# Decoder step: one weight transfer order, new-token values and sigmoid placement changed

## The reference

```python
mod = (silu(c) @ w_ada + b_ada)               # six shift/scale/gain vectors
h = x * (1 + sc1) + sh1
qa, ka, va, qb, kb, vb, ga, gb = split(h @ w_in)
# branch A: three groups of dilated attention, merged by their softmax denominators; branch B: block attention
# for a sample row the keys and values are [cached rows, the 4 new rows of its own sequence]
oa, ob = mixer(q, k, v)                        # 4 heads x 64 each
merged = sigmoid(ga) * (oa @ w_pa) + sigmoid(gb) * (ob @ w_pb)
x = layer_norm(ALPHA * x + g1 * (merged @ w_o))
f = (silu(gt) * up) @ w_down                   # up, gt = split(h2 @ w_up)
y = layer_norm(ALPHA * x + g2 * f)
```

## Time and profile before

| | |
|---|---|
| median of 3 runs | 548.4 us (546.83 to 549.36) |
| the profiled execution | 547.36 us, its span 545.8 us, TensorE's mean granted clock 0.981 |
| TensorE matmul busy | 505.8 us, 93% |
| VectorE, ScalarE, GpSimd busy | 290.1 (53%), 223.0 (41%), 89.0 us (16%) |
| chain that ended last | TensorE 76%, DMA 10%, VectorE 4%, SP's queue 3% |
| moved by DMA | 116.75 MB, 214 GB/s over the span |

### The profile page before, as it was taken

The page is one execution under the profiler, slowest core; times in us unless marked ns, Lnnn a source line. Parts: engine busy times, 40 slices in busy tenths (PEclk is TensorE's granted clock), DMA queues, the critical chain, the costliest instruction groups (busy, mean ns, idle before and its releaser), DMA issues.

```text
span 545.8 us, 9902 instructions
## 1 busy us (share of the span) xinstructions
PE 505.8 (93%) x3859; PEld 460.2 (84%) x3859; DVE 290.1 (53%) x548; ACT 223.0 (41%) x370; POOL 89.0 (16%) x127
## 2 busy tenths in 40 slices
PE   3989999998999799998999799999999999999980
PEld 1578988888788698895999599999999999999980
DVE  0266675757435354343875767545544544346356
ACT  1145333315434544356434455464444443333311
POOL 1000111126900000000244408210011100000005
PEclk9999999999999899999999889999999999999996
DMA  8999995495768920655443717997678754354002
GB/s 272 406 409 373 392 323 203 161 375 161 260 217 253 344 81 1 202 189 177 133 143 98 248 54 236 366 317 249 230 253 262 266 190 162 115 180 169 1 0 86
DMA packets 81356, 116.75 MB, mean 214 GB/s; under 512 B 3595, under 2 KB 59083, under 8 KB 80804
## 3 DMA queue, kind: packets, MB, share of 16 engines
q1 hardware_dynamic: 79428, 102.76, 55.4%
q0 software_dynamic: 1888, 13.44, 6.9%
HBM read 112.90 MB, written 13.57 MB: 232 GB/s over the span
## 4 chain that ended last, share of the span: by engine, by line
PE 76%; DMA 10%; DVE 4%; SPq 3%; issue 2%; ACT 2%; POOL 1%; POOLq 0%; ACTq 0%; DVEq 0%
PE psum L721 21%; PE psum L723 19%; PE psum L722 19%; DMA raw<-in_w_in 6%; DMA raw<-in_w_up 4%; PE psum L742 3%; PE psum L871 3%; PE psum L987 2%; PE psum L973 1%; DMA ada_s<-in_w_ada 1%; PE psum L756 1%; ACT w_hi L484 1%; PE psum L931 1%; PE psum L940 1%; PE psum L885 1%
## 5 line engine op out<-in xcount | busy, mean ns | idle before, releaser
L489 DVE TENSOR_TENSOR w_lo<-raw,w_hi 128x1024 fp32r<-128x1024 f32 (+1 forms) x120 | 147.0, 1227 | 157.2 <-ACT w_hi L484 156.8
L721 PE MATMUL psum<-act_hi,w_hi 128*128 128x288 f32 x736 | 223.2, 303 | 7.1 <-DVE act_lo L1753 2.9
L722 PE MATMUL psum<-act_lo,w_hi 128*128 128x288 f32 x736 | 218.4, 297 | 0.0
L723 PE MATMUL psum<-act_hi,w_lo 128*128 128x288 f32 x736 | 217.8, 296 | 0.0
L484 ACT ACTIVATE w_hi<-raw 128x1024 fp32r<-128x1024 f32 (+1 forms) x120 | 124.6, 1041 | 121.9 <-PE psum L723 93.2
L721 PEld LDWEIGHTS psum<-act_hi,w_hi 128*128 128x128 f32 x736 | 139.4, 189 | 20.2 <-issue 14.3
L723 PEld LDWEIGHTS psum<-act_hi,w_lo 128*128 128x128 f32 x736 | 139.8, 190 | 0.0
L722 PEld LDWEIGHTS psum<-act_lo,w_hi 128*128 128x128 f32 x736 | 139.7, 190 | 0.1
L721 PE MATMUL psum<-f_hi,w_hi 128*128 128x288 f32 x176 | 52.4, 298 | 0.6 <-DVE f_t L1790 0.6
L722 PE MATMUL psum<-f_lo,w_hi 128*128 128x288 f32 x176 | 51.9, 295 | 0.0
L723 PE MATMUL psum<-f_hi,w_lo 128*128 128x288 f32 x176 | 51.8, 294 | 0.0
(11 more groups left out here) (194 smaller groups left out, 560.7 us busy)
## 6 DMA issues: line engine op xcount, KB each, us to landing
raw<-in_w_up SPq DMA_DIRECT2D x22, 1024.0 KB, 5.8
ada_s<-in_w_ada SPq DMA_DIRECT2D x20, 1024.0 KB, 10.4
raw<-in_w_in SPq DMA_DIRECT2D x17, 1024.0 KB, 7.8
raw<-in_w_down SPq DMA_DIRECT2D x10, 1024.0 KB, 5.1
out<-in_cache_kv_a POOLq DMA_DIRECT2D x16, 504.0 KB, 6.4
raw<-in_w_ada SPq DMA_DIRECT2D x4, 1024.0 KB, 6.7
raw<-in_w_o SPq DMA_DIRECT2D x4, 1024.0 KB, 4.9
raw<-in_w_in SPq DMA_DIRECT2D x4, 768.0 KB, 12.9
```

What stands on the lines that cost most here:

```text
L489: nc.vector.tensor_tensor(part(w_lo, slot4, by_rows), raw_half(rslot, hh, by_rows), part(w_hi, slot4, by_rows).bitcast(F32), ALU.subtract) ...
L721: nc.tensor.matmul(out, hi_l, hi_r, start=start, stop=False, skip_group_check=True)
L722: nc.tensor.matmul(out, hi_l, lo_r, start=False, stop=False, skip_group_check=True)
L723: return nc.tensor.matmul(out, lo_l, hi_r, start=False, stop=stop, skip_group_check=True)
```

## The change

Four things change. (1) In SP's queue `GATE0 + 2` goes ahead of the keys of sequence 5, `GATE0 + 3` and `GATE0 + 4` go ahead of the values of sequence 0, `GATE0 + 5` ahead of the values of sequence 2, and `GATE0 + 6` ahead of a wait for GpSimd's stores and the values of sequences 3 and 4. (2) The new tokens' sample values are multiplied once, in a step 11 (`sample_new`), and their rows are picked by a third 0/1 table. (3) VectorE adds the three picked parts, so TensorE gathers one part in 4 matmuls; `own_rows` runs in steps 9, 12 and 14, and in step 14 ahead of `out_copy`. (4) ScalarE makes the first sigmoids after step 15 and puts the three copies of outputs between sigmoids. The table of constants is 4 columns wider.

```diff
--- before.py
+++ after.py
@@ -116,7 +116,7 @@
 C_MB1 = C_MA0 + 384
 C_EPS = C_MB1 + 256
 C_SELM = C_EPS + 1
-C_SEL = C_SELM + 8
+C_SEL = C_SELM + 12
 C_W32 = C_SEL + SAMPLE
 C_END = C_W32 + 32
 
@@ -138,6 +138,7 @@
     c[:, C_W32:C_W32 + 32] = 1.0 / 32
     b, h, t = row_of(np.arange(128))
     c[:, C_SELM:C_SELM + 8] = (b // 4 * 4 + h)[:, None] == np.arange(8)[None, :]
+    c[:, C_SELM + 8:C_SELM + 12] = h[:, None] == np.arange(4)[None, :]
     c[:, C_SEL:C_SEL + SAMPLE] = (b * DEC_T + t)[:, None] == np.arange(SAMPLE)[None, :]
     return c
 
@@ -393,7 +394,7 @@
     tok_turned, v_tok, k_tok = sem("tok_turned"), sem("v_tok"), sem("k_tok")
     kt_turned, kt_x, kt_y, scored_s = sem("kt_turned"), sem("kt_x"), sem("kt_y"), sem("scored_s")
     max_s, exp_s, prob_s = sem("max_s"), sem("exp_s"), sem("prob_s")
-    probT_turned, probT_s, pv_s = sem("probT_turned"), sem("probT_s"), sem("pv_s")
+    probT_turned, probT_s, pv_s, own_added = sem("probT_turned"), sem("probT_s"), sem("pv_s"), sem("own_added")
     scored, maxed, exped, turned, prbT_a, prbT_b, pv_done, o_ready = (sem(n) for n in (
         "scored", "maxed", "exped", "turned", "prbT_a", "prbT_b", "pv_done", "o_ready"))
     oT_turned, oT_h, oT_l = sem("oT_turned"), sem("oT_h"), sem("oT_l")
@@ -664,22 +665,23 @@
         load_kv(3, 0)
         sp.wait_ge(tok_turned, 11)
         load_kv(4, 0)
+        load_static(GATE0 + 2)
         for b in range(5, DEC_B):
             sp.wait_ge(kt_turned, b)
             load_kv(b, 0)
-        load_static(GATE0 + 2)
+        load_static(GATE0 + 3)
+        load_static(GATE0 + 4)
         for b in range(2):
             sp.wait_ge(kt_turned, 14 + b)
             load_kv(b, 1)
-        load_static(GATE0 + 3)
+        load_static(GATE0 + 5)
         sp.wait_ge(scored_s, 4)
         load_kv(2, 1)
-        load_static(GATE0 + 4)
+        load_static(GATE0 + 6)
         sp.wait_ge(stored_k, 16 * N_POOL_STORES)
         load_kv(3, 1)
-        load_static(GATE0 + 5)
         load_kv(4, 1)
-        for n in range(GATE0 + 6, PAB0 + 1):
+        for n in range(GATE0 + 7, PAB0 + 1):
             load_static(n)
         sp.wait_ge(pv_s, 1)
         for b in range(5, DEC_B):
@@ -915,14 +917,18 @@
                 if n in (3, 7, 9):
                     mm.then_inc(probT_turned, 1)
 
+        def sample_new():
+            pe.wait_ge(masked_s, 1)
+            for g in range(4):
+                mm = nc.tensor.matmul(psum[:, 7, 256 * (g // 3):256 * (g // 3) + 256], s_prbT[0:SAMPLE, 6 + g, :],
+                                      tok[0:SAMPLE, 2, 1, 256 * g:256 * g + 256], start=(g == 0), stop=(g >= 2),
+                                      skip_group_check=True)
+            mm.then_inc(pv_s, 1)
+
         def sample_values(half):
 
             if half == 1:
-                pe.wait_ge(masked_s, 1)
-            for g in range(4):
-                nc.tensor.matmul(psum[:, 7, 256 * (g // 3):256 * (g // 3) + 256], s_prbT[0:SAMPLE, 6 + g, :],
-                                 tok[0:SAMPLE, 2, 1, 256 * g:256 * g + 256], start=(g == 0), stop=False,
-                                 skip_group_check=True)
+                pe.wait_ge(masked_s, 2)
             for q in range(4):
                 place, before = kv_place(4 * half + q, 1)
                 pe.wait_ge(kv_in[place], 16 * KV_LOADS * (before + 1))
@@ -930,7 +936,7 @@
                 for q in range(4):
                     mm = nc.tensor.matmul(psum[32 * q:32 * q + 32, 7, 256 * br:256 * br + 256],
                                           s_prbT[0:nr, n, 32 * q:32 * q + 32], kv_tiles(4 * half + q, 1, tile)[0:nr, 0, :],
-                                          start=False, stop=(n == 5), skip_group_check=True)
+                                          start=(n == 0), stop=(n in (3, 5)), skip_group_check=True)
             mm.then_inc(pv_s, 1)
 
         def score(u, i, n):
@@ -1014,17 +1020,17 @@
                 prompt_values(s - 4)
             if s in (8, 13):
                 sample_values(s // 13)
+            if s == 11:
+                sample_new()
             if s == 14:
                 pe.wait_ge(o_ready, 8)
                 pe.wait_ge(maxed, 16)
                 outputs_turn(0)
 
-        pe.wait_ge(masked_s, 2)
+        pe.wait_ge(own_added, 1)
         for f in range(4):
-            for half in range(2):
-                mm = nc.tensor.matmul(psum[:, 7, SAMPLE * f:SAMPLE * f + SAMPLE], o_masked[:, half, 128 * f:128 * f + 128],
-                                      cst[:, C_SEL:C_SEL + SAMPLE], start=(f == 0 and half == 0), stop=(half == 1),
-                                      skip_group_check=True)
+            mm = nc.tensor.matmul(psum[:, 7, SAMPLE * f:SAMPLE * f + SAMPLE], o_masked[:, 0, 128 * f:128 * f + 128],
+                                  cst[:, C_SEL:C_SEL + SAMPLE], start=(f == 0), stop=True, skip_group_check=True)
         mm.then_inc(sel_done, 1)
 
         ada_ring(pe, ADA1)
@@ -1318,15 +1324,9 @@
                 softmax_exp(s - 2)
             if 3 <= s < N_UNITS + 3:
                 prbT_copy(s - 3)
-            if s == 14:
-                act.wait_ge(acc_free[0], 18)
-                act.wait_ge(acc_free[1], 18)
-                sigmoids(22, 24)
-                sigmoids(28, 32)
-            if s == 15:
-                sigmoids(12, 14)
-                sigmoids(24, 28)
-                sigmoids(14, 18)
+        act.wait_ge(acc_free[0], 18)
+        act.wait_ge(acc_free[1], 18)
+        sigmoids(22, 24)
 
         def oT_leading(br):
             act.wait_ge(oT_turned, br + 1)
@@ -1338,8 +1338,12 @@
         act.wait_ge(sel_done, 1)
         nc.scalar.activation(oT_hi[:, :, PROMPT:TOK], psum[:, 7, 0:4 * SAMPLE].rearrange("p (k c) -> p k c", c=SAMPLE),
                              ACT.Copy).then_inc(oT_h, 1)
+        sigmoids(28, 32)
         oT_leading(1)
+        sigmoids(12, 14)
+        sigmoids(24, 28)
         ada_rows(10)
+        sigmoids(14, 18)
         for h in range(4):
             hi_static(act, H_PAB + h + AHEAD)
             if h % 2 == 1:
@@ -1643,16 +1647,25 @@
                                       small[:, 96 + r0 + i:97 + r0 + i], None, ALU.mult)
             ins.then_inc(o_ready, 1)
 
-        def own_rows(half):
-
-            dve.wait_ge(pv_s, half + 1)
-            if half == 0:
+        def own_rows(part):
+
+            dve.wait_ge(pv_s, part + 1)
+            if part == 0:
                 dve.wait_ge(scored, scored_by(7))
-            pick = cst[:, C_SELM + 4 * half:C_SELM + 4 * half + 4].unsqueeze(2).broadcast_to([128, 4, E])
+            c = C_SELM + (0, 8, 4)[part]
+            pick = cst[:, c:c + 4].unsqueeze(2).broadcast_to([128, 4, E])
+            dst = min(part, 1)
             for br in range(2):
-                ins = V.tensor_tensor(o_masked[:, half, 256 * br:256 * br + 256].rearrange("p (j e) -> p j e", e=E),
+                ins = V.tensor_tensor(o_masked[:, dst, 256 * br:256 * br + 256].rearrange("p (j e) -> p j e", e=E),
                                       psum[:, 7, 256 * br:256 * br + 256].rearrange("p (j e) -> p j e", e=E), pick, ALU.mult)
             ins.then_inc(masked_s, 1)
+            if part > 0:
+                dve.wait_ge(masked_s, part + 1)
+                ins = V.tensor_tensor(o_masked[:, 0, :], o_masked[:, 0, :], o_masked[:, 1, :], ALU.add)
+                if part == 2:
+                    ins.then_inc(own_added, 1)
+                else:
+                    link(ins)
 
         def oT_rest(br):
             dve.wait_ge(oT_h, 1 if br == 0 else 3)
@@ -1672,11 +1685,13 @@
                 softmax_max(s - 2)
             if 3 <= s < N_UNITS + 3:
                 prbT_copy(s - 3)
+            if s == 14:
+                own_rows(2)
             if s >= 4:
                 out_copy(s - 4)
             if s == 9:
                 own_rows(0)
-            if s == 14:
+            if s == 12:
                 own_rows(1)
         oT_rest(0)
         dve.wait_ge(oT_h, 2)
```

## The result

| | before | change |
|---|---|---|
| median | 547.99 us (546.83 to 549.36, 4 runs) | 541.01 us (539.16 to 543.92, 4 runs) |
| ratio, 95% interval | | 0.9876, 0.9842 to 0.991 |
| profiled execution | 547.36 us | 540.16 us, its span 538.6 us |
| mean granted clock | 0.981 | 0.980 |

The change is faster, by 7.0 us on the medians; the forecast was 540.6. Over all executions, those timed later too, the mean is 540.13 us for the change (16) and 547.90 for before (60), 7.8 us apart.

The account below looks back on a forecast made before the run. TensorE, busy 93% of the span, was taken to bound the kernel. Terms of -3.5, -1.4, -1.9, -0.95, -1.4, +0.95 and +0.4 sum to -7.8 us, giving 540.6 us on the median, range 537.5 to 544.5.

Parts of the forecast that it names:

- (a): TensorE's wait for the first probabilities: with gate weights issued earlier it goes entirely, -3.5 us.
- (b): Gate products behind the wait for the first probabilities: TensorE's half clock there goes, -1.4 us.
- second rival: First probabilities: ScalarE's and VectorE's order, not the weight transfer, makes the softmax late; 545.5 us, chance 6%.
- (c): Sample products of steps 8, 11 and 13: new tokens' values multiplied once, one of two groups goes, -1.9 us.
- (d): Gather of sample outputs on TensorE: one part gathered, 8 of 16 passes stay, -0.95 us.
- (e): Before the first products with w_pa: output copies between sigmoids end TensorE's wait, -1.4 us.
- first rival: Behind the first w_pa products: VectorE's and ScalarE's own order takes the last gain back; 542.0 us, chance 13%.
- (f): Before prompt_values(11): VectorE's picking ahead of out_copy(10) makes TensorE go later, +0.9 us (0.94).
- third rival: Behind the idle before prompt_values(11): a new stretch at half clock loses 2.0 us; 542.6 us, chance 8%.
- (g): Key turns: keys of sequences 5 to 7 queue behind a 1 MB block, +0.4 us, bounds nothing and 2.9.
- So the block fits, but hardly: DMA between 137 and 143: room for 1.28 MB takes GATE0 + 2 ahead of the keys of sequences 5 to 7.
- last rival: Key turns: three gate blocks share DMA, keys up to 8.7 us late with half clock; 553.1 us, chance 3%.

Follow-up runs that it names:

- queue order alone: The kernel before with only the change's new order of weight blocks in SP's queue; 544.42 us, ratio 0.9935.
- the part alone: The change with SyncE's and ScalarE's programs as before, so only the sample products and VectorE's part changed; 546.48 us, ratio 0.998.
- ScalarE's order alone: The kernel before with only ScalarE's sigmoids moved so that output copies go between them; 547.86 us, ratio 1.0.
- two ahead: The change with GATE0 + 3 also ahead of the keys of sequences 5 to 7; 548.38 us, ratio 1.0009.
- the keys first: The change with GATE0 + 2 back behind the keys of sequence 7, GATE0 + 3 and + 4 right behind it; 541.24 us, second time 539.48 us.
- the addition behind: The change with VectorE's last addition of picked parts put behind out_copy(10); 540.31 us, second time 540.09 us.

## Why the prediction was right, point by point

(a), (b) **Right.** -3.5 and -1.4 predicted, -3.6 and -1.5 in the trace, and queue order alone gives the same to 0.02 us. How near (a) came is in part luck: the wait it removes was 3.47, 3.37 and 2.29 us in the three profiles with before's order of the gate blocks. The softmax was not late by itself (second rival): with `GATE0 + 4` early the probabilities came in time in every kernel that had it. The half clock behind the wait went with the wait.

(c) **Right in size**, -1.9 predicted and -1.8 measured. The moved group costs 2.06 us in step 11, where it had cost 1.92; step 13 with 1.92 us less cover did not wait. In the times of the part alone it can't be told from nothing.

(d), (e) **Right.** -0.95 and -1.4 predicted, -2.4 together in the trace; ScalarE's order alone gives -1.5. The first rival (the gain taken back behind the first products) is refuted: the stage behind kept its length to 0.03 us with or without it.

(f) **Mechanism right, the term too large by a quarter of a us; a stretch at half clock follows in part of the executions.** The way to the gather grew by 0.69 us where 0.94 was predicted; the wait is the 1.1 us of the list. The addition took 0.69, as the row it was priced by. VectorE's row of work took 2.07 us (245.10 to 247.17) where 2.15 was reckoned, it began 0.14 us after TensorE's last turn where 0.23 was reckoned, and the gather followed the start of the values after 0.47 us where before had 0.57; these three make up the 0.25. The wait became 1.08 where about 1.2 was said. But in four of seven profiles a stretch at half clock followed, which took another 1.5 us. That is what the third rival describes, with a chance of 8% and a price of 2.0; it came more often than that and cost a little less, though that the wait alone brings it isn't shown. Where it came, the profiled executions (538.88 to 540.90 us) stayed inside the range.

(g) **The step that was mis-sized: "So the block fits, but hardly".** In the change's own profiles it cost 0.1, 0.0 and 0.3 us where 0.4 was forecast, which is right. In two of six profiles with that queue order it cost 6.1 and 5.7 us, and the upper bound, 2.9, was too low; a wait for keys of 2 us or more was the prediction's own sign of being wrong. The bound took the block's time at the full rate, for all transfers alike, and looked at the keys of sequence 7. The runs showed the keys of sequence 5, right behind the block, to be the ones that decide, with one transfer that took 9.2 us to land while its neighbours took 5.2 to 6.2, and a half clock behind the wait that cost another 1.7 us each time. The DMA engines were full from 143 on already before (share 1.06 in the window 143 to 146), so the room of 1.28 MB, a mean over the 6 us ahead, said little. The last rival, keys late, was put at 3% and at three blocks; two ahead suffice (all 12 executions took over 546.5 us), one does in part of them. That the usual case cost next to nothing was better in luck than in reasons: in the change this transfer landed as TensorE asked for it.

That the time came out 0.4 us from the forecast is good aim in the terms and chance in the rest. (a) to (e), which carry the sum, each held to 0.2 us; with (f) and (g) smaller than forecast the touched stages gave -8.6 us in the trace where the sum has -7.8. The profile's own start and end gave 1.3 us of that back, and over all executions it is 7.8 us, which holds the low clock behind the wait in some of them. The two terms that add time hold as a usual case; their tails were larger than their bounds.

## To carry to other kernels

A transfer of 1 MB may be late for what waits for it because of its place in the queue, and moving it up is worth the wait and the slow clock behind it. Try first the place behind the small transfers that are used as they land: here the gain of 5 us came whole with the keys first. One block ahead of them was followed by 4 us of waiting for a single transfer in two of six profiles, two blocks by 6 us. That the keys first is safe from this isn't shown. Work added to an engine off the critical path belongs behind the one instruction that the bound engine waits for. And a change of parts is read in the trace between the same two instructions of the bound engine, since parts of 1 to 2 us can't be told by medians of runs that spread by 2 to 3 us.

## What the runs showed of the hardware

TensorE's clock fell to its half (1.2 of 2.4 GHz) in two places where nothing idle stood before: in the sample products of ScalarE's order alone (0.70, then 0.50 in the windows above), and in step 11 of the second run of the addition behind. Both falls came right behind the eight passes of the new tokens' values (K = 32), and each cost about 1.5 us. In 15 other places the same passes brought none, so what brings a fall is left open.

A wait of about 1 us was followed by the low clock in four profiles of seven at the same place, and in two of three of the same kernel, so one profile doesn't tell what a wait costs.

With the DMA engines full (a share of 1.04 to 1.06 from 146 to 155 in the two profiles with late keys), one transfer of 128 KB took 9.2 us to land, in both at the same place in the queue, while the other five of `in_cache_kv_b` in each of the two took 4.1 to 7.7 us.
